# A window-attention stage on one Trainium2 core: key transposes in two halves, with the scores between them

## The reference

```python
def dilated_window_attention(qg, k_all, v_all, q_off):
    ...
        for g, (win, dil) in enumerate(DILATED_GROUPS):   # (128,1), (512,4), (2048,16)
            n_keys = win // dil + 1
            idx = rows[:, None] - dil * jnp.arange(n_keys, dtype=jnp.int32)[None, :]
            ...
            s = jnp.einsum('bqhd,bqjhd->bqhj', qb[:, :, g], kg).astype(jnp.float32) * scale
            s = jnp.where(valid[None, :, None, :], s, -jnp.inf)
            lse = jax.nn.logsumexp(s, axis=-1)
            p = jnp.exp(s - lse[..., None])
            outs.append(jnp.einsum('bqhj,bqjhd->bqhd', p, vg.astype(jnp.float32)))
            ...
        wgt = jax.nn.softmax(jnp.stack(lses, axis=0), axis=0)
        o = jnp.sum(wgt[..., None] * jnp.stack(outs, axis=0), axis=0)
```

## Time and profile before

| | |
|---|---|
| time, median of 3 runs | 2580.54 us (2576.63 to 2580.55) |
| the profiled execution | 2582.86 us |
| its span in the trace | 2581.1 us |
| PE busy | 2517.5 us (98%) |
| DVE busy | 1313.0 us (51%) |
| ACT busy | 563.4 us (22%) |
| chain that ended last | PE 92%; DMA 2%; ACT 2%; DVE 2% |
| mean granted TensorE clock | 0.995 |

### The profile page before, as it was taken

One profiled execution on the slowest core, in us unless ns is written; L12 is line 12 of the kernel. 1 busy time (PEld: TensorE's weight loads), 2 busy tenths in 40 slices (PEclk: granted clock), 3 DMA queues, 4 the chain that ended last, 5 costly groups with the idle time before them and its releaser, 6 DMA issues.

```text
span 2581.1 us, 52968 instructions
## 1 busy us (share of the span) xinstructions
PE 2517.5 (98%) x23108; PEld 2052.3 (80%) x23108; DVE 1313.0 (51%) x2839; ACT 563.4 (22%) x1257; POOL 67.7 (3%) x92
## 2 busy tenths in 40 slices
PE   7999999999999999999999999999999999999998
PEld 6999856666666768999999997566666566789998
DVE  5663554335542472766376635533455334636654
ACT  2110231123432222211111111311344222221011
POOL 0000000000000110000000000000000001100000
PEclk9999999999999999999999999999999999999999
DMA  7445569642986556444534456685439765564443
GB/s 233 146 119 146 211 235 341 229 147 94 385 324 244 151 214 245 132 153 114 165 117 153 113 172 234 236 318 198 166 130 393 276 226 176 211 222 133 131 113 88
DMA packets 260709, 505.66 MB, mean 196 GB/s; under 512 B 9792, under 2 KB 198720, under 8 KB 245376
## 3 DMA queue, kind: packets, MB, share of 16 engines
q1 hardware_dynamic: 251776, 330.83, 38.9%
q0 software_dynamic: 8704, 171.45, 18.1%
HBM read 491.95 MB, written 140.85 MB: 245 GB/s over the span
## 4 chain that ended last, share of the span: by engine, by line
PE 92%; DMA 2%; ACT 2%; DVE 2%; issue 1%; PEld 1%; SPq 0%; DVEq 0%; ACTq 0%
PE ps L736 87%; PE ps L739 5%; DMA big<-in_cache_swa_k_dram 2%; PEld ps L736 1%; ACT big L1884 0%; DMA ring<-in_f_wu_dram 0%; ACT reg L1884 0%; DVE reg L2052 0%; DVE reg L2126 0%; DVE x L2044 0%; DVE reg L2644 0%; DVE ring L2565 0%; DVE reg L2615 0%; ACT big L1634 0%; ACT L1843 0%
## 5 line engine op out<-in xcount | busy, mean ns | idle before, releaser
L736 PE MATMUL ps<-reg 128*128 128x160 f32 (+12 forms) x4584 | 516.4, 294 | 1.6 <-DVE reg L2131 1.6
L736 PEld LDWEIGHTS ps<-reg 128*128 128x128 f32 (+5 forms) x4584 | 455.8, 163 | 34.6 <-issue 25.2
L736 PE MATMUL ps<-h,ring 128*128 128x320 f32 (+2 forms) x1984 | 448.8, 378 | 14.6 <-DMA ring<-in_f_wu_dram 13.6
L736 PE MATMUL ps<-reg,ring 128*128 128x160 f32 (+1 forms) x3040 | 458.9, 306 | 0.0
L736 PEld LDWEIGHTS ps<-reg,ring 128*128 128x128 f32 x3040 | 426.1, 189 | 16.4 <-issue 6.2
L736 PEld LDWEIGHTS ps<-h,ring 128*128 128x128 f32 (+1 forms) x1984 | 323.0, 189 | 105.1 <-issue 26.7
L736 PE MATMUL ps<-ring,h 128*128 128x512 f32 (+3 forms) x896 | 250.9, 472 | 0.0
L736 PEld LDWEIGHTS ps<-big,ring 128*128 128x128 f32 (+2 forms) x2016 | 198.2, 168 | 33.7 <-issue 29.4
L736 PE MATMUL ps<-big,ring 128*128 128x160 f32 (+2 forms) x2016 | 216.0, 280 | 8.0 <-issue 7.5
L736 PEld LDWEIGHTS ps<-ring,h 128*128 128x128 f32 (+1 forms) x896 | 102.4, 163 | 79.9 <-issue 64.5
L736 PE MATMUL ps<-big,reg 32*64 32x256 f32 (+8 forms) x2144 | 133.2, 348 | 4.3 <-issue 4.3
(11 more groups left out here) (322 smaller groups left out, 2659.9 us busy)
## 6 DMA issues: line engine op xcount, KB each, us to landing
out_o_swa_k_s_dram<-in_cache_swa_k_dram POOLq DMA_DIRECT2D x16, 4080.0 KB, 15.5
out_o_swa_v_s_dram<-in_cache_swa_v_dram POOLq DMA_DIRECT2D x16, 4080.0 KB, 16.8
ring<-in_w_in_dram SPq DMA_DIRECT2D x30, 2048.0 KB, 8.7
ring<-in_f_wd_dram SPq DMA_DIRECT2D x32, 1408.0 KB, 7.0
ring<-in_f_wg_dram SPq DMA_DIRECT2D x42, 1024.0 KB, 5.5
ring<-in_f_wu_dram SPq DMA_DIRECT2D x42, 1024.0 KB, 8.2
big<-in_cache_swa_k_dram SPq DMA_DIRECT2D x32, 1024.0 KB, 8.7
ring<-in_cache_swa_v_dram SPq DMA_DIRECT2D x32, 1024.0 KB, 7.6
```

The source lines that it names most:

```text
L736: return pe.matmul(out, lhsT, rhs, start=first, stop=last, skip_group_check=True)
```

## The change

`transposes` gets the groups that it is to turn. The first part is turned whole as before. In the loop groups 0 and 1 of part `n + 1` are turned ahead of `scores(n)` as before, and groups 2 and 3 behind it. Nothing else is changed: the instructions are the same in number and form, and the streams of ACT, DVE, SP and POOL are the same.

```diff
-                def transposes(n):
+                def transposes(n, chunks):
 
                     b, part = n // 3, n % 3
                     pe.wait_ge(s_kw[part], 16 * (b + 1))
-                    for c in range(4):
+                    for c in chunks:
                         if c >= 2:
                             pe.wait_ge(S["kt_act"], 3 * n + c - 1)
                         elif n:
...
-                transposes(0)
+                transposes(0, range(4))
                 for n in range(3 * NB + 6):
                     b, part = n // 3, n % 3
                     if n + 1 < 3 * NB:
-                        transposes(n + 1)
+                        transposes(n + 1, (0, 1))
                     if part == 2 and b >= 2:
                         by_channel(b - 2)
                     if n < 3 * NB:
                         scores(n)
+                    if n + 1 < 3 * NB:
+                        transposes(n + 1, (2, 3))
                     if part == 0 and b >= 2:
```

## The result

The changed kernel takes 2592.4 us in the median of 10 runs (2587.1 to 2601.9), the kernel before 2580.6 beside it (10 runs, 2574.5 to 2588.7). The ratio is 1.0046 with a 95% interval of 1.0031 to 1.0061: slower by 11.9 us, where +9.7 was forecast. The profiled execution took 2591.2, its span is 2589.4.

What follows compares the result with a forecast made beforehand. PE, busy 98% of the span, was taken as the bound. Gaps removed (1.26 us a period) against new switches and waits gave +0.69 a period, +4.8 a layer; 2580.5 + 9.7 = 2590 us, range 2584 to 2598.

Steps and rivals of the forecast that it cites:

- S0 to S1: From a sample's part 0 scores to its part 1 scores: 3.55 us, including 0.37 waiting for VectorE's group 3 copy.
- S1 to S2: From a sample's part 1 scores to its part 2 scores, with the values product between: 5.64 us.
- The switch from transposes to the values product: A new PE switch in part 1, in no row of the trace: taken at 0.11 us, bounds 0 and 0.21.
- S2 to S0: From part 2 scores to the next sample's first scores: 5.05 us, the delayed masked row costing 1.31.
- Head: From the stage's first transpose to sample 1's first scores: 15.62 us against 15.55, +0.07 a layer.
- Sample 1: The stage's second sample period, with no values yet: 11.35 us against 10.65, +0.70 a layer.
- Last sample: From the last sample's part 0 scores to its part 2 scores: 8.90 us against 7.80, +1.10 a layer.
- The sum: Head, sample 1, five full periods (+2.96) and last sample: +4.8 us a layer, +9.7 for both.
- The key loads: SP's key loads start later, part 1 tightest: costed at nothing; 0.3 late at every part 1 would be some 4 us.
- The clock rival: Masked-row waits among the stage's transposes lower PE's clock: one to four falls, +1.5 to +6 us; 15% together with late loads.
- The rule against the rows: Skill's 275 ns per transpose, taken as spacing in a row: no gaps to remove, +7 us; the rows' 0.117 us was used.
- The faster rival: In the stage, PE's three gaps go without VectorE's waits: period 12.5, -14 us, 2566; half the waits, -2 us; chance 6%.

Runs made afterwards that it cites:

- small-load pair: Changed kernel and kernel before, each loading only part of the keys from the second sample on: 2591.8 against 2583.8 us.
- the kernel with part 2's place whole: Changed kernel with transposes ahead of a sample's last scores turned whole again, split only at parts 0 and 1: ratios 1.0042 and 1.0028 in two runs.
- halves at parts 1 and 2, result first: Changed kernel with groups 2 and 3 behind scores of parts 1 and 2 only, VectorE's result ahead of its group 3 copy: 2580.3 us, ratio 0.9996.

## Why the prediction was right

**The place and the kind of the loss** were right: VectorE's queue, with the copy of group 3 ahead of the result and the masked row. Point by point, from the rows of after:

- S0 to S1: 3.55 predicted, 3.56 measured (697.90 to 701.46), with the wait for the copy of 0.33 at group 1.
- S1 to S2: 5.64, measured 5.62 (to 707.08). The switch from transposes to the values product, which no row of before showed, costs 0.11: four transposes at 0.117 are 0.47, and the product starts 0.58 after them (702.72 to 703.30). It was taken at 0.11.
- S2 to S0: 5.05, measured 5.00 (to 712.08). The masked row starts 3.02 after S2, predicted 3.07. The waits were put at 0.9 in sum before the shares and 0.4 at S0; the profile's idle times are 0.70 and 0.43, and the start before the shares is later by 0.83 than eight transposes in a row would have it (708.82 + 0.47 = 709.29 to 710.12).
- Head, first transpose to S0 of sample 1: 15.62; in the trace 642.47 to 658.15 = 15.68. Here the wait for the masked row is 1.30. Sample 1: 11.35, measured 11.39. Last sample: 8.90, measured 8.93.

```profile
642.47 1.09 PE L739 MATMUL ps<-cst,big 128*128 128x128 f32 x8
...
658.15 1.33 PE L736 MATMUL ps<-reg 128*16 128x512 f32 x24 [1.30 <-DVE sml L2646]
...
669.54 1.33 PE L736 MATMUL ps<-big,reg 128*16 128x512 f32 x24 [0.92 <-DVE sml L2646]
...
735.24 1.20 PE L739 MATMUL ps<-cst,big 128*128 128x128 f32 x9 [0.87 <-DMA big<-in_cache_swa_k_dram]
...
741.37 1.33 PE L736 MATMUL ps<-reg 128*16 128x512 f32 x24 [0.43 <-DVE sml L2646]
...
750.30 0.88 PE L736 MATMUL ps<-reg 128*16 128x256 f32 x40
```

**The sum.** The stage up to the last scores is 107.83 in the first layer of after and was 102.24: +5.6, of which 0.9 is the one late load at 735.24, so 4.7 for the 4.8 predicted. In the second layer it is 107.36 against 103.36, only +4.0, because before had a gap of 1.2 there in which nothing was waited for. Together +9.6, for +9.7. That closeness is in part luck: the head and the five periods of before were taken with their own late loads in them (15.55 and 68.24), and without them, in the small-load pair, the same steps cost 5.3 and 5.5 a layer, 10.7 in all. The medians of that pair differ by 8.0, those of the full kernels by 11.9; the forecast lies between, and nothing finer can be told from whole times.

**The key loads** were costed at nothing and cost 0.9 us once in the profile. That is inside the range that was kept for them, though a wait of PE for key loads was named as a sign of being wrong. It was also not at part 1, which the prediction held for the tightest, but at part 0, whose transposes start at 735.24 behind the values product. The 1.1 us of such waits given for before are of the first layer; both layers have 2.0.

**The clock rival** was met in kind, not as priced. The wait of 1.30 for the first sample's masked row was followed by no slower rows, and the waits of the periods by none either. At the end of the first layer's stage, behind the same wait as before (1.29 there), the granted clock fell to the lower level, where the profile of before had it in the second layer:

```profile
756.00:758.00 2.00, 2.00 (x12) 1.21 (x10) 1.58 (x9) 0.00 (x0) 0.00 (x0) 0.50 0.70 285
2037.00:2039.00 2.00, 2.00 (x25) 1.18 (x28) 1.71 (x9) 0.00 (x0) 0.00 (x0) 1.00 0.82 336
```

Both falls lie behind the last sample's scores, and each of the two profiles has such a fall once, so it makes no difference between them. At that place it comes and goes, also without the change: the kernel before with small loads had it in both layers, the changed one with small loads in neither. A fall ahead of a stage's last scores stands in one profile only, of the kernel with part 2's place whole: behind a gap of 2.02 us in which nothing was waited for, the level was 0.50 at 732 to 734 us.

**The rule against the rows** (the Trainium skill, "TensorE: Matmul & The Clock Gate", "Part 4: PE-mode transpose", some 275 ns each) is settled as far as the spacing goes: taken as that, it left no gaps ahead of group 2 to remove, and they did go. As the length of one transpose the trace agrees with it: a row of eight lasts 1.09, which is seven spacings of 0.117 and 0.27.

**The faster rival** was right about its condition. Where VectorE is out of the way (halves at parts 1 and 2, result first) the period falls to 12.92 where no load is late, but the loads, not VectorE, then took the gain.

## What to carry to other kernels

When work is moved back in one engine's order, look at what the engine behind it has queued after that work's consumer. Eight transposes moved past a sample's last scores cost PE nothing by themselves (with this place alone in halves the period grew by 0.40: the later start of the shares, 0.83, less the gap of 0.42 that went); they made a copy on VectorE late, and the copy held back, by order alone, two steps that did not depend on it and that PE needed soon. Then ask what the next bound allows before hunting the gap: here the loads left half a us a period at most, by the estimate above, so that even the right order brought nothing that could be measured.

## What the runs showed of the hardware beyond that

PE had 9 to 21 us of gaps at matmuls in each profile, up to 3.4 us each, in which the profile shows nothing waited for; their number and place differ from execution to execution of the same kernel (20.6 and 12.7 us in two). That is as much as the whole effect that was studied, and a reason to compare starts within a stage and not spans. Within a stage the starts repeat to 0.01 us where no such gap and no late load falls: four periods of the changed kernel in a row were 14.18, 14.18, 14.18 and 14.17.
